# First block's gates and short convolution as pairs of seven half products, with x kept in memory meanwhile

## The chip, the cores and the metric

The program runs on one core of a Trainium2 chip. Its time is the device time of one execution in microseconds; of several executions the median is given. The engines are TensorE (PE: matmuls, with PEld for its weight loads), VectorE (DVE), ScalarE (ACT), GpSimd (POOL) and SyncE (SP), which here only issues transfers. Each engine runs its own instructions in order and waits for the others on semaphores.

## What is computed

Two transformer blocks of width 1024 over 1024 positions. The first block normalizes x, projects it (`w_in`) to the features of an RWKV-7 recurrence, of a short convolution and of two gates, and merges the two branches:

```python
out_a = rwkv7_branch(...)            # scan, then a group norm per head of 64, bonus, gate
u = cg * xc                          # short_conv_branch
out_b = bg * conv3(u, conv_w)        # causal, depthwise, width 3
merged = (sigmoid(ga + bg_a) * (out_a @ w_proj_a) + sigmoid(gb + bg_b) * (out_b @ w_proj_b))
x = x + merged @ w_out_mix
```

`ga` and `gb` have 1024 columns each, `bg`, `cg` and `xc` 512 each. Attention to a memory and an MLP follow, and then the second block.

## The kernel before

Activations lie transposed: a tile is 128 features by 1024 positions, in two halves of 512 (`HALF`). For precision every operand of a large product is split in two parts, `hi` (rounded) and `lo` (the remainder), and a product is three matmuls: hi by w_hi, lo by w_hi, hi by w_lo. A weight tile is 128 output columns by 1024 inputs (`KT` = 8 k-steps of 128), so a plain tile is 8 x 3 x 2 = 48 matmuls of 512 columns (`Weights.multiply`, line 280). GpSimd splits a weight tile (`split_tile`: `w_hi` at line 161, `w_lo` at line 164) after its transfer has landed and its slot is free.

In the first block the order is: features (`rwkv_features`, four turns of three tiles), the scan (`rwkv_scan`), and then the stage that changes. `gates` runs 16 plain tiles (for each of `ga` and `gb` eight) and applies the sigmoid out of PSUM (line 2744) to two buffers that are stored to memory. Its first tile is multiplied at the end of the scan's block (`multiply_early`). Beside it `RwkvOutput` finishes the scan's output in eight halves: TensorE sums over heads (lines 2412 and 2418, full precision), VectorE centres, takes a reciprocal (2445) and scales (2447 to 2455), ScalarE squares, takes the root (2430) and rounds. `ShortConv` follows in the same block: 12 plain tiles, in four turns of `cg`, `xc` and `bg`. Then `merge` multiplies both branches by their projections; its weights and the stored gates come in on the sync queue (`fetch`, `load_gates`, line 3277). `add_product` adds the last product to x, which stays in on-chip memory (`x_t`) all the time.

Other stages already use seven half products instead of eight for a pair of tiles (a Winograd form of Strassen's scheme): the MLP, and the second block's gates, `pair_gates`. There two tiles of 128 columns by 1024 inputs are a 2 x 2 block matrix with the halves of the inputs, as are the activations with the halves of the inputs and of the positions. Four sums of the activations' blocks are formed once (`HalfSums`: t1 on GpSimd, lines 2852 to 2860; t2, t3 and t4 on VectorE in PSUM, lines 2885 to 2895, rounded by ScalarE). Four sums of weight blocks per pair are formed by GpSimd (`sum_into`, line 823), every operand is rounded by ScalarE (`round`, line 807) and its remainder taken by GpSimd (`rest`, line 818) into a ring of five slots. A product is 4 k-steps x 3 = 12 matmuls (line 859), a pair 84. Between products ScalarE copies and VectorE adds partial results between PSUM banks (`seed_u`, `keep_fifth`, `seed_last`, `add_fifth`, `end_fifth`). `EarlyPart` multiplies just 2 of the 8 k-steps of the first tile before the block boundary.

Blocks (`nc.Block`) are separated by a barrier of all engines; semaphores can be cleared between them (`clear_and_free_semaphores`).

## Time and profile before

| what | us |
|---|---|
| median of 3 runs | 2989.02 (2986.13 to 2990.33) |
| profiled execution, its time | 2989.97 |
| its span, first to last instruction | 2988.2 |
| TensorE busy | 2863.9 |
| stage of gates and short convolution on TensorE | 499.83 to 819.94 |

The profile is of one execution. TensorE's mean granted clock in it is 0.989 of full speed. Times of rows are microseconds from the start of the span; a bracket gives the idle time before an instruction and who ended it.

### The profile page before, as it was taken

Reading aid. Unit: us, or ns where it says so; the run is one execution under the profiler, and the core shown is the slowest. Engines: PE = TensorE matmul, PEld = TensorE weight load, DVE = VectorE, ACT = ScalarE, POOL = GpSimd, SP = SyncE. Lnnn points to the kernel's source line nnn. Section 1 sums busy time; section 2 is a strip of 40 time slices with the busy share of each in tenths; the row PEclk is TensorE's granted clock in tenths of the full one; section 3 lists DMA queues with packets and bytes.
Section 4 is the critical chain, followed back from the end, with each engine's and each line's share of the span. In section 5 each row is a group of like instructions: output and inputs, shape, how many; then the busy total and the mean of one; then the engine's idle time right before and its main releaser. Section 6 shows DMA issues by size and latency. Waiting matters only on the chain. (4 is left out here: it accounts for less than half of the span.)

```text
span 2988.2 us, 48247 instructions
## 1 busy us (share of the span) xinstructions
PE 2863.9 (96%) x20146; PEld 2292.3 (77%) x20146; DVE 1476.3 (49%) x1739; ACT 950.9 (32%) x1455; POOL 1139.7 (38%) x807
## 2 busy tenths in 40 slices
PE   7999788999999999999999999999999799999999
PEld 6777677778878876788888888777877678866677
DVE  6454442423464434543333333777578436357661
ACT  5433232321011123422222222433233335567400
POOL 1331222444344430344444444211121457645552
PEclk9999999999999999999999999999999999999999
DMA  6232433442142111111111111122333534322143
GB/s 212 84 127 102 110 100 84 124 127 81 28 141 71 50 50 41 38 43 57 57 57 57 50 50 50 29 78 72 99 92 98 167 106 127 117 96 64 61 141 127
DMA packets 310864, 258.38 MB, mean 86 GB/s; under 512 B 47010, under 2 KB 269401, under 8 KB 310666
## 3 DMA queue, kind: packets, MB, share of 16 engines
q1 hardware_dynamic: 310410, 255.48, 28.3%
q8 instruction: 149, 2.44, 0.3%
q14 instruction: 49, 0.40, 0.0%
q10 hardware_dynamic: 256, 0.07, 0.0%
HBM read 191.79 MB, written 63.31 MB: 85 GB/s over the span
## 5 line engine op out<-in xcount | busy, mean ns | idle before, releaser
L280 PE MATMUL ps<-h_hi,w_hi 128*128 128x512 f32 x1376 | 444.2, 404 | 6.3 <-POOL w_lo L177 3.7
L280 PE MATMUL ps<-h_lo,w_hi 128*128 128x512 f32 x1376 | 426.4, 391 | 0.0
L280 PE MATMUL ps<-h_hi,w_lo 128*128 128x512 f32 x1376 | 425.1, 390 | 0.0
L161 POOL TENSOR_TENSOR w_hi<-w_raw,ones 128x1024 fp32r<-128x1024 f32 x78 | 189.3, 2427 | 475.8 <-PE ps L280 322.4
L818 POOL TENSOR_TENSOR op_lo<-w_raw,op_hi 128x512 fp32r<-128x512 f32 x160 | 205.8, 1291 | 371.8 <-ACT op_hi L807 371.2
L280 PEld LDWEIGHTS ps<-h_hi,w_hi 128*128 128x128 f32 x1376 | 256.7, 188 | 85.4 <-issue 31.0
L280 PEld LDWEIGHTS ps<-h_hi,w_lo 128*128 128x128 f32 x1376 | 259.4, 189 | 55.3
L280 PEld LDWEIGHTS ps<-h_lo,w_hi 128*128 128x128 f32 x1376 | 259.1, 188 | 55.3
L164 POOL TENSOR_TENSOR w_lo<-w_raw,w_hi 128x1024 fp32r<-128x1024 f32 x78 | 203.8, 2613 | 6.1
L1367 DVE TENSOR_TENSOR x_t<-x_t,ps 128x512 f32<-128x512 f32 x128 | 87.6, 687 | 223.2 <-PE ps L859 207.3
L177 POOL TENSOR_TENSOR w_lo<-w_raw,w_hi 128x1024 fp32r<-128x1024 f32 x30 | 73.1, 2438 | 303.6 <-ACT w_hi L172 303.6
L859 PE MATMUL ps<-hid_hi,op_hi 128*128 128x512 f32 x448 | 174.3, 389 | 0.0
L859 PE MATMUL ps<-hid_lo,op_hi 128*128 128x512 f32 x448 | 174.3, 389 | 0.0
L859 PE MATMUL ps<-hid_hi,op_lo 128*128 128x512 f32 x448 | 174.3, 389 | 0.0
L807 ACT CAST op_hi<-w_raw 128x512 fp32r<-128x512 f32 x155 | 95.6, 621 | 192.8 <-PE ps L859 158.2
L280 PE MATMUL ps<-branch_hi,w_hi 128*128 128x512 f32 x384 | 119.4, 392 | 5.8 <-POOL w_lo L164 2.1
L4561 DVE RECIPROCAL p_root<-p_root 128x1024 f32<-128x1024 f32 x16 | 104.8, 6547 | 36.3 <-ACT p_root L4415 36.1
L280 PE MATMUL ps<-branch_lo,w_hi 128*128 128x512 f32 x384 | 118.3, 389 | 0.0
L280 PE MATMUL ps<-branch_hi,w_lo 128*128 128x512 f32 x384 | 118.3, 389 | 0.0
L5389 POOL TENSOR_TENSOR sb_weight<-sb_weight,sb_left 128x512 f32<-128x512 f32 (+3 forms) x96 | 84.9, 896 | 71.2 <-DVE sb_left L5543 70.6
L5543 DVE TENSOR_TENSOR_SCAN sb_left<-ps,sb_left,ones 128x512 f32<-128x512 f32 (+3 forms) x96 | 92.4, 1004 | 34.2 <-ACT ps L5489 32.5
L859 PE MATMUL ps<-h_hi,op_hi 128*128 128x512 f32 x256 | 99.8, 390 | 0.0
(640 smaller groups left out, 5940.8 us busy)
## 6 DMA issues: line engine op xcount, KB each, us to landing
w_raw<-in_w_in_dram SPq DMA_DIRECT2D x91, 512.0 KB, 4.8
w_raw<-in_w_up_dram SPq DMA_DIRECT2D x32, 512.0 KB, 4.0
w_raw<-in_w_down_dram SPq DMA_DIRECT2D x32, 512.0 KB, 3.4
kv_raw<-in_w_kv_dram SPq DMA_DIRECT2D x16, 512.0 KB, 5.1
mix_gates<-mix_sig SPq DMA_DIRECT2D x16, 512.0 KB, 3.0
mix_gate_b<-mix_gates SPq DMA_DIRECT2D x32, 256.0 KB, 4.3
mix_gates<-mix_sig SPq DMA_DIRECT2D x32, 256.0 KB, 2.5
x_in<-in_x_dram SPq DMA_DIRECT2D x8, 512.0 KB, 8.9
```

The lines of the kernel that those rows point to most:

```text
L161: pool.tensor_tensor(c.w_hi[:, s], c.w_raw[:, s], c.ones[:].unsqueeze(1).broadcast_to([P, KT, P]), ALU.mult).then_inc(c.w_rounded, 1)
L164: pool.tensor_tensor(c.w_lo[:, s], c.w_raw[:, s], c.w_hi[:, s].bitcast(F32), ALU.subtract).then_inc(c.w_split, 1)
L177: eng.tensor_tensor(c.w_lo[:, s], c.w_raw[:, s], c.w_hi[:, s].bitcast(F32), ALU.subtract).then_inc(c.w_split, 1)
L280: last = pe.matmul(o, w[:, s, k], a[:, k - offset, (half + h) * width:(half + h + 1) * width], start=(k == kts[0] and w is c.w_hi and a is ...
L807: act.copy(self.hi(o)[:], src).then_inc(self.rounded, 1)
L818: pool.tensor_tensor(self.lo(o)[:], src, self.hi(o)[:].bitcast(F32), ALU.subtract).then_inc(self.pooled, 1)
L859: last = pe.matmul(out, w[:, k], a(k), start=start and k == 0 and w is w_hi and a is hi, stop=stop and k == HK - 1 and w is w_lo, skip_gro ...
L1367: dve.tensor_tensor(c.x[:, n, half[h]], c.x[:, n, half[h]], ps[:, bank_of(g, n, place)], ALU.add).then_inc(down_free, 1)
L4561: v.mark(dve.reciprocal(root[:], root[:]))
L5389: pool.tensor_tensor(weight[:, n % 4, hd, 0:width], weight[:, n % 4, hd, 0:width], left[:, n % 2, hd, 1:width + 1], ALU.mult).then_inc(wei ...
L5543: dve.tensor_tensor_scan(l[:, hd, 0:width][:, ::-1], ps[:, 2 * (n % 2) + hd, 0:width][:, ::-1], c.ones[:, 0:1].broadcast_to([P, width]), l ...
```

## The change

The 28 tiles of the stage become four plain gate tiles and 24 tiles in twelve pairs of seven half products, six pairs of gate tiles and six of convolution tiles (`cg` with `xc` twice, then two `bg` tiles, and all again). `first_gates` takes the place of `gates` and `ShortConv`. Its half sums t2 and t3 need the room of x, so x is stored to memory in the features stage (two tiles a turn, ahead of the turn's weight fetches) and loaded again during the merge's first turns; t1 is rounded in place of a quarter of the activations, once the last plain tile has read it (`h12_read`). The splits of t1 are issued within the first pair. The scan's output is finished beside the plain tiles (halves 0 and 1) and the six gate pairs (one half each). The taps' accumulator is in PSUM. The merge's block is preceded by a clearing of semaphores, and `add_product` waits for x tile by tile.

```diff
--- before.py
+++ after.py
...
                 weights.done(dve, k // 2, k % 2)
+                dve.wait_ge(c.x_back, 16 * (k + 1))
                 dve.tensor_tensor(c.x[:, k], c.x[:, k], c.ps[:, 2 * (k % 2):2 * (k % 2) + 2, :].rearrange("p b n -> p (b n)"),
                                   ALU.add).then_inc(free[k % 2], 1)
...
+                    for n in range(2 * i, 2 * i + 2):
+                        sp.dma_start(c.scratch["x_spill"][n], c.x[:, n]).then_inc(c.x_spilled, 16)
                     fetch(i, 0)
                     fetch(i, 1)
...
-class ShortConv:
...
-def gates(c, name, w_in, first_column, bias):
...
@@ -2816,7 +2601,10 @@
         self.rest(pool, o)
         self.sum_into(pool, s3, a21, a11, ALU.subtract, count + self.SUM1)
         self.sum_into(pool, s2, s3, a22, ALU.add, count + self.SUM4)
-        for m in (1, 2, 3, 4):
+        first_sums()
+        self.rest(pool, o + 1)
+        before_third()
+        for m in (2, 3, 4):
             self.rest(pool, o + m)
...
+            t[1] = [buf[:, 0:HK, HALF:SEQ] for buf in (c.h_hi, c.h_lo)]
+        self.raw = [c.nc.alloc_sbuf_tensor_at(f"{name}_t1raw{m}", [P, HALF], F32, offset=off) for m, off in enumerate(raw)]
...
+def first_gates(c, w_in, bias):
...
+    gate_tile_of, conv_tile_of = tile_of(w_in, RWKV_COLS + 3 * D_RWKV), tile_of(w_in, RWKV_COLS)
+    weights = EarlyPart(c, [lambda i, u=u: gate_tile_of(0, 1, u // 2 + (u % 2) * KT) for u in range(4)], 1)
...
+        x_base, tail_base = c.h_base - BRANCH, aux + 2 * BRANCH
+        gate_tiles = [gate_tile_of(0, 1, 2 * i + k + g * KT) for i in range(1, 4) for g in range(2) for k in range(2)]
+        conv_order = [(o, i) for two in range(2) for o, i in ((1, 2 * two), (2, 2 * two), (1, 2 * two + 1), (2, 2 * two + 1),
+                                                              (0, 2 * two), (0, 2 * two + 1))]
+        s = PairStream(c, "gate_op", gate_tiles + [conv_tile_of(0, 1, o * CT + i) for o, i in conv_order], ring=(0, 2, 1, 4, 3), shift=0)
+        n_gates, n_pairs = len(gate_tiles) // 2, s.pairs
+        t = HalfSums(c, name, {2: x_base, 3: x_base + 16384, 4: tail_base},
+                     [aux + 28672, aux + 30720, aux + BRANCH + 24576, aux + BRANCH + 26624], banks={3: 5, 2: 6, 4: 7}, inplace=True)
...
+        with nc.Block() as block:
...
+                s.fetch(sp, 2)
+                side.load(sp, 1)
+                store_tile(0)
+                sp.wait_ge(c.w_split, weights.t0 + 3)
+                s.fetch(sp, 0)
+                sp.wait_ge(c.w_split, weights.t0 + 4)
+                s.fetch(sp, 1)
+                store_tile(1)
...
+                for p in range(n_pairs):
+                    s.fetch(sp, 2 * p + 3)
+                    if p < n_gates:
+                        store_quarter(p, 0)
+                        side.load(sp, p + 3)
+                    s.fetch(sp, 2 * p + 4)
...
+            @block.gpsimd
+            def _(pool):
+                t.pool_form(pool, 0)
+                t.pool_form(pool, 1)
+                weights.split_tile(pool, 0, 2)
+                t.pool_form(pool, 2)
+                weights.split_tile(pool, 0, 3)
+                t.pool_form(pool, 3)
+                weights.done(pool, 0, 2)
+                def first_sums():
+                    for j in range(HK):
+                        t.pool_split(pool, j)
+                s.pool_products(pool, 0, first_sums, lambda: weights.done(pool, 0, 3))
+                for p in range(1, n_pairs):
+                    s.pool_products(pool, p)
...
+                for u in range(2):
+                    pool.wait_ge(s.used, s.total - 3 + 3 * u)
+                    following.split_tile(pool, 0, u)
+                following.ahead = 2
...
+                    out_banks = [ps[:, 2 * (u % 2)], ps[:, 2 * (u % 2) + 1]]
+                    weights.ready(pe, 0, u)
+                    wait(pe, gated, u - 1)
+                    if u == 0:
...
+                        weights.part(pe, out_banks, c.h_hi, c.h_lo, range(HK), u).then_inc(h12_read, 1)
+                        last = weights.part(pe, out_banks, c.h_hi, c.h_lo, range(HK, KT), u)
+                    else:
+                        last = weights.multiply(pe, u, out_banks, c.h_hi, c.h_lo, before=between(u))
+                    last.then_inc(c.tile_done, 1)
...
+                    if gates_now and p:
+                        side.pe_means(pe, n)
+                    if p == 0:
+                        pe.wait_ge(side.rooted, 2)
+                    elif p == n_gates:
+                        pe.wait_ge(side.rooted, 2 * CT)
+                    else:
+                        bank_free(0)
+                    s.product(pe, o, ps[:, A], *b11).then_inc(s.used, 1)
+                    if p:
+                        bank_free(1)
+                    else:
+                        pe.wait_ge(gated, 3)
+                    s.product(pe, o + 1, ps[:, E], *t.at(1), before=after_split(1)).then_inc(s.used, 1)
+                    if gates_now and p > 1:
+                        side.pe_spreads(pe, n)
+                    pe.wait_ge(xcopied, 3 * p + 1)
+                    s.product(pe, o + 2, ps[:, B], *t.at(2), start=False, before=after_split(2)).then_inc(s.used, 1)
...
+                        pe.wait_ge(t.split[3], HK)
+                        side.pe_means(pe, n)
+                    if p == 1:
+                        side.pe_spreads(pe, n)
+                    s.product(pe, o + 3, ps[:, A], *b21, start=False).then_inc(s.used, 1)
...
+                t.act_begin(act, 0)
+                t.act_round(act, 3, 0)
+                t.act_round(act, 2, 0)
+                t.act_round(act, 4, 0)
+                t.act_begin(act, 1)
+                gate_tile(0)
+                side.act_square(act, 0)
+                t.act_round(act, 3, 1)
+                t.act_round(act, 2, 1)
+                side.act_root(act, 0)
+                t.act_round(act, 4, 1)
+                t.act_begin(act, 2)
+                gate_tile(1)
+                side.act_late(act, 0)
+                side.act_square(act, 1)
+                t.act_round(act, 3, 2)
+                t.act_round(act, 2, 2)
+                t.act_round(act, 4, 2)
+                t.act_begin(act, 3)
+                side.act_root(act, 1)
+                gate_tile(2)
+                for m in (0, 1):
+                    s.round(act, m)
+                for j in range(HK):
+                    if j == 0:
+                        act.wait_ge(h12_read, 1)
+                    if j == HK - 1:
+                        t.act_round(act, 3, 3)
+                    act.wait_ge(t.formed[3], j + 1)
+                    t.act_round(act, 1, j)
+                t.act_round(act, 2, 3)
+                t.act_round(act, 4, 3)
+                weights.done(act, 0, 3)
+                s.round(act, 2)
+                gate_tile(3)
+                s.round(act, 3)
...
+                    o, n = s.PAIR_OPS * p, p + 2
+                    if p > 1:
+                        side.act_square(act, n)
+                    seed_u(p)
+                    s.round(act, o + 4)
+                    keep_fifth(p)
+                    if p == 1:
...
+                    s.round(act, o + 6)
+                    if p == 0:
+                        side.act_late(act, 1)
+                    gate_quarter(p, 0)
...
+                    if p:
+                        side.act_late(act, n)
+                    gate_quarter(p, 1)
+                    s.round(act, o + 9)
...
+                def add_fifth(p):
+                    A, E, B, C, DD = banks(p)
+                    dve.wait_ge(s.used, s.PAIR_OPS * p + 3)
+                    dve.wait_ge(xcopied, 3 * p + 2)
+                    if p <= n_gates:
+                        dve.wait_ge(gated, gates_until(p - 1, 2 if p else 3))
+                    else:
+                        dve.wait_ge(free[2], p - n_gates)
+                    dve.tensor_tensor(ps[:, C], ps[:, B], fifth[:], ALU.add).then_inc(xadded, 1)
...
+                        u, acc = u_in[h], ps[:, 6 + h]
+                        v.mark(dve.tensor_scalar(acc, u[:, 2:HALF + 2], vec(c, "conv_w", i + 2 * CT), None, ALU.mult))
+                        for tap in (1, 0):
+                            v.wait(dve)
+                            ins = dve.scalar_tensor_tensor(out=acc if tap else y[:, i, half[h]], in0=u[:, tap:HALF + tap],
+                                                           scalar=vec(c, "conv_w", i + tap * CT), in1=acc, op0=ALU.mult, op1=ALU.add)
+                            v.mark(ins)
+                    v.wait(dve)
+                    dve.sem_inc(ended, 1)
...
+                def gate_y(p, m):
+                    n, h, product = places[m]
+                    i = conv_at(p, n)[1]
+                    finished(p, m)
+                    dve.tensor_tensor(y[:, i, half[h]], y[:, i, half[h]], ps[:, bank(p, m)], ALU.mult).then_inc(made, 1)
+                    dve.wait_ge(made, 4 * ((p - n_gates) // 3) + m + 1)
+                    dve.sem_inc(free[m], 1)
...
+                dve.wait_ge(c.x_spilled, 16 * KT)
+                dve.memset(u_in[0][:, 0:2], 0.0).then_inc(padded, 1)
+                form(0, 3, 2, 4)
+                split_t(0, 3, 2, 4)
+                side.dve_centre(dve, 0)
+                form(1, 3, 2, 4)
+                split_t(1, 3, 2, 4)
+                side.dve_invert(dve, 0)
+                side.dve_apply(dve, 0)
+                side.dve_finish(dve, 0)
+                side.dve_centre(dve, 1)
+                form(2, 3, 2, 4)
+                split_t(2, 3, 2, 4)
+                form(3, 3, 2, 4)
+                split_t(3, 3, 2, 4)
+                side.dve_invert(dve, 1)
+                side.dve_apply(dve, 1)
+                for p in range(n_gates):
+                    n = p + 2
...
+                    if products_of(p):
+                        gate_y(p, 0)
+                        end_fifth(p)
+                        gate_y(p, 1)
+                        split_y(p, 0)
+                        gate_y(p, 2)
+                        split_y(p, 1)
+                        gate_y(p, 3)
+                        split_y(p, 2)
+                        split_y(p, 3)
+                    else:
+                        end_fifth(p)
+                        scale_u(p, 1)
+                        scale_u(p, 3)
+                        taps(p)
+    return weights, build
...
+            nc.clear_and_free_semaphores(c.done_with)
+            c.stage_sems = [s for s in c.stage_sems if s not in c.done_with]
         with nc.Block() as block:
...
                             fetch(i, u)
                         load_gates(i + 1, u)
+                        for k in range(4 * i + 2 * u, 4 * i + 2 * u + 2) if x_back and i < 2 else ():
+                            sp.dma_start(c.x[:, k], c.scratch["x_spill"][k]).then_inc(c.x_back, 16)
                 sp.wait_ge(c.w_split, weights.t0 + weights.total)
                 following.load_first(sp)
...
 def first_block(c):
     d = c.dram
+    scratch(c, "x_spill", [KT, P, SEQ])
     loras, lora_tail = start_to_loras(c)
+    c.x_spilled, c.x_back = c.sem("x_spilled"), c.sem("x_back")
     feature_weights, features = rwkv_features(c)
     loras(feature_weights)
     scan_in = ScanInputs(c)
     features(scan_in, lora_tail)
-    gate_weights, gate = gates(c, "mix", d["w_in"][0], RWKV_COLS + 3 * D_RWKV, "b_gate")
+    gate_weights, gate = first_gates(c, d["w_in"][0], "b_gate")
     rwkv_scan(c, gate_weights, scan_in)
     c.br_hi = at(c, 0, "branch_hi", [P, KT, SEQ], F32R)
     c.br_lo = at(c, BRANCH, "branch_lo", [P, KT, SEQ], F32R)
-    side = RwkvOutput(c)
     merge_weights, merge_1 = merge(c, "mix", d["w_proj_a"][0], d["w_proj_b"][0])
-    sig = [at(c, BRANCH + 4 * (CT + n) * SEQ, f"mix_sig{n}", [P, SEQ])[:] for n in range(2)]
-    gate(side, sig, after=ShortConv(c, side, merge_weights))
+    gate(merge_weights)
     out_weights = residual_weights(c, d["w_out_mix"][0])
-    merge_1(out_weights)
+    merge_1(out_weights, x_back=True)
     h, branches = (c.h_hi, c.h_lo), (c.br_hi, c.br_lo)
     query_weights, query = queries(c)
     late = LateNorm(c, "norm_xattn", query_weights, branches, "norm_xattn")
```

## Rows read from the trace of the kernel before

**Rows 1.** Page, busy us, share of the span, instructions.
```profile
PE 2863.9 (96%) x20146; PEld 2292.3 (77%) x20146; DVE 1476.3 (49%) x1739; ACT 950.9 (32%) x1455; POOL 1139.7 (38%) x807
```

**Rows 2.** Timeline of TensorE through the stage: start, us, engine, line, operation, count.
```profile
499.83 0.73 PE L280 MATMUL ps<-h_hi,w_hi 128*128 128x512 f32 x2
...
510.39 0.61 PE L280 MATMUL ps<-h_hi,w_lo 128*128 128x512 f32 x2
511.33 0.70 PE L280 MATMUL ps<-h_hi,w_hi 128*128 128x512 f32 x2 [0.32 <-PEq L1935]
...
642.69 1.04 PE L280 MATMUL ps<-h_hi,w_hi 128*128 128x512 f32 x2
643.56 0.62 PE L280 MATMUL ps<-h_lo,w_hi 128*128 128x512 f32 x2
...
718.85 0.62 PE L280 MATMUL ps<-h_hi,w_lo 128*128 128x512 f32 x2
...
730.18 0.62 PE L280 MATMUL ps<-h_hi,w_hi 128*128 128x512 f32 x2
...
819.94 0.62 PE L280 MATMUL ps<-branch_hi,w_hi 128*128 128x512 f32 x2
```

**Rows 3.** Busy time by stretch (columns in the first line), one pair, second gates.
```profile
core 0: us, PE busy (x) PEld busy (x) DVE busy (x) ACT busy (x) POOL busy (x), PEclk, DMA share, GB/s
2560.20:2581.10 20.90, 20.90 (x101) 17.54 (x100) 7.45 (x10) 12.34 (x19) 14.37 (x11) 1.00 0.43 127
```

**Rows 4.** Timeline of TensorE, boundary before the second block's gates.
```profile
2469.83 0.70 PE L2909 MATMUL ps<-h_hi,w_hi 128*128 128x512 f32 x2 [1.00 <-PEq L4750]
```

**Rows 5.** Timeline of VectorE and GpSimd, half sums of the second gates.
```profile
2470.43 0.70 DVE L2887 TENSOR_TENSOR ps<-ps,h_lo 128x512 f32<-128x512 f32 x1 [3.80 <-ACT ps L2865]
...
2476.78 0.68 DVE L2895 TENSOR_TENSOR mix_t4lo<-ps,mix_t4hi 128x512 fp32r<-128x512 f32 x1
...
2483.26 2.54 POOL L2860 TENSOR_TENSOR mix_t1lo<-mix_t1raw,mix_t1hi 128x512 fp32r<-128x512 f32 x2
```

**Rows 6.** Timeline of ScalarE and VectorE, first half of the scan's output.
```profile
519.26 1.28 ACT L2430 ACT_TABLE_LOAD   x1
...
522.52 3.35 DVE L2445 RECIPROCAL ro_root<-ro_root 128x512 f32<-128x512 f32 x1 [6.37 <-ACT ro_root L2430]
525.91 1.71 DVE L2447 TENSOR_TENSOR ro_dev<-ro_dev,ro_root 128x512 f32<-128x512 f32 x1
527.66 2.50 DVE L2449 TENSOR_SCALAR ro_dev<-ro_dev,vec 128x512 f32<-128x512 f32 x1
```

**Rows 7.** Timeline of TensorE behind a wait in the memory keys.
```profile
72.45 0.73 PE L3599 MATMUL ps<-kv_hi,mem_hi 128*128 128x512 f32 x2 [2.43 <-DVE kv_lo L3589]
...
77.36 0.61 PE L3599 MATMUL ps<-kv_hi,mem_lo 128*128 128x512 f32 x2
```

**Rows 8.** Busy time by stretch, the same place.
```profile
74.00:76.00 2.00, 2.00 (x6) 1.52 (x6) 2.00 (x3) 0.71 (x2) 0.00 (x0) 0.50 1.19 297
```

**Rows 9.** Timeline of SyncE, GpSimd and TensorE, the merge's fifth tile.
```profile
855.26 0.38 SPq L124 DMA_DIRECT2D w_raw<-in_w_proj_a_dram  x1
...
861.02 2.39 POOL L161 TENSOR_TENSOR w_hi<-w_raw,ones 128x1024 fp32r<-128x1024 f32 x1 [13.31 <-DMA w_raw<-in_w_proj_b_dram]
863.49 2.39 POOL L164 TENSOR_TENSOR w_lo<-w_raw,w_hi 128x1024 fp32r<-128x1024 f32 x1
...
866.13 0.70 PE L280 MATMUL ps<-branch_hi,w_hi 128*128 128x512 f32 x2 [0.77 <-DVE mix_gate_a L3351]
```

**Rows 10.** DMA view of 848 to 866 us, in 40 slices.
```profile
GB/s 0 0 27 123 314 269 173 341 373 378 300 32 0 0 214 355 305 305 296 337 328 249 307 340 325 133 22 93 264 223 109 178 173 319 287 264 273 296 346 344
DMA packets 3522, 4.06 MB, mean 225 GB/s; under 512 B 239, under 2 KB 1985, under 8 KB 3521
```

**Rows 11.** Waits of TensorE, whole span: us in total, times, longest.
```profile
PE ps L4305 <- PEq L5558: 1.6, 1, 1.6
```

**Rows 12.** Waits of TensorE, 2500 to 2642 us.
```profile
PE ps L2498 <- ACT do_sq L2490: 0.8, 1, 0.8
```

**Rows 13.** Groups by shape, 497 to 865 us: busy us, mean ns; idle before.
```profile
L2634 DVE TENSOR_TENSOR branch_lo<-conv_y,branch_hi 128x512 f32 x6 | 12.4, 2105 | 1.2 <-ACT branch_hi L2600 1.2
```

554 lines of the change are left out of this document (323 added, 231 removed).

## Prediction

> **What bounds the kernel now.** I read the engine shares first: TensorE is busy for 96% of the span, so time is won by giving it less work and lost wherever it is made to wait [rows 1]. Then I read its timeline through the stage that changes. The stage starts at 499.83 us, when the first gate tile is multiplied behind the scan, and ends at 819.94 us, when the merge's first product starts: 320.1 us [rows 2]. Between 718.85 and 730.18 us there are 50 matmuls of 512 columns, so one costs 0.2266 us. The stage has 28 tiles (16 gate, 12 convolution) of 8 k-steps, 3 products and 2 halves: 1344 matmuls, 304.6 us. The 16 full-precision sums of the scan's output cost more: the pair that holds one takes 0.87 us instead of 0.45, and the sum itself 0.45, so 0.87 each, 13.9 us. One block boundary adds 0.49 us (510.39 + 0.45 to 511.33). Together 319.0 of 320.1 us: TensorE never waits here for another engine. Third, the second block's gates: they already run as plain tiles and then six pairs of seven half products, which makes them the measured model of the new stage.
>
> **What the change removes.** Four plain tiles are 192 matmuls; 24 tiles in 12 pairs are 12 x 7 products x 4 k-steps x 3 = 1008. That is 1200 in place of 1344: 144 fewer at 0.2266 = **-32.6 us**. The 16 sums stay.
>
> **Whether the pairs keep pace.** A pair of the other gate stage takes 20.90 us with TensorE busy throughout, 84 x 0.2266 = 19.0 plus its side work; GpSimd is busy for 14.4 us of it, ScalarE 12.3, VectorE 7.5 [rows 3]. The new gate pairs last 19.0 + 2 x 0.87 = 20.8, the convolution pairs 19.0. GpSimd's eleven operations (7 remainders, 4 sums; 14.37 / 11 = 1.3 us each) fit either. In a gate pair VectorE gets a 3.35 us reciprocal and about 3 to 6 us of scaling where the model had 0.2 us; that is about 12 of 20.8 us, and the bank it releases last (the fifth quarter) is wanted only three products (8.2 us) later. A convolution pair gives VectorE six tap operations; their accumulator lies in PSUM, where operations took 0.70 us beside GpSimd [rows 5], so about 5 us, over before the next pair's addition is due at 8.2 us. I cost the 12 pairs at no stall; if the cover were gone, each microsecond per pair would be 12 us.
>
> **The start of the stage.** Until now a whole tile (10.9 us) was multiplied before the block boundary and covered it. Now only 2 of 8 k-steps are (12 matmuls, 2.7 us), as in the other stage, where TensorE waited 1.00 us at the boundary [rows 4] against 0.32 here; the last store of the scan must land as well, so I take **+1.0** rather than 0.7 (bounds 0.6 to 2).
> After it (call this T) TensorE has 36 + 144 matmuls and four sums, so pair 0 could begin at T+44.3. VectorE has to form and split the half sums in that time. In the model one of four rounds took 7.05 us (2470.43 to 2477.46) [rows 5], so 28 us. But it also has two halves of the scan's output to finish: a reciprocal of 3.35 us and four scalings, of which the first two took 1.71 and 2.50 us while GpSimd worked [rows 6]. I walk the written order with these durations: sums 0 until T+8; centring 0 at 9.3, behind TensorE's sum; sums 1 until 19.0, because ScalarE's root with its 1.28 us table load stands between its roundings; reciprocal until 22.4; scaling beside GpSimd until 29.5; finishing and centring 1 until 32.2; sums 2 until 39.4; sums 3 until 44.5. ScalarE waits for these: its last `act_begin` ends at 39.1, root 1 at 41.1, the gate of tile 2 with another table load at 43.5, the rounding of weight 0 at 44.1. Only then can GpSimd go on: remainder 0 (45.4), two sums (48.0), **four splits of the first half sum, now inside the first pair** (two took 2.54 us in the model [rows 5], so 5.1; 53.0), remainder 1 (54.3). TensorE begins product 0 at 45.4, is done at 48.1 and waits for remainder 1 until 54.3. Against a start at T+44.3 and product 1 at 47.0 this is 7.3 us, of which about 0.6 is the second spread sum waiting for ScalarE's square. The walk takes the slowed scalings at their slowest, so I take **+6.5** (bounds: 1, if VectorE's scalings are not slowed and ScalarE gains what it loses to table loads; 12).
> A wait of that kind has an after-effect in this trace: behind a 2.43 us wait the granted clock went from full to 0.50 (1.2 GHz), and 14 matmuls took 4.91 us instead of 3.17 [rows 7, 8]. **+1.7** (0 to 3).
> What else is queued there: product 2 needs the second half sum (split by 47) and its seed copy (51), so nothing is late next; the first pair's addition meets a VectorE that is still scaling until about 58, when product 2 ends at 60.
>
> **The copies of x.** Eight stores of 512 KB in the features stage go on the sync queue ahead of weight fetches whose tile is due a whole turn (three tiles) later: 0. Reading back is another matter. The sync queue issues two loads of 512 KB (x0, x1) after the gate loads of tile 2 of the merge and two more (x2, x3) just ahead of the weights of tile 4, which before were issued at 855.26, landed at 861.0, were split by 865.88, and TensorE started on them at 866.13: it was already waiting for exactly this chain [rows 9]. In that stretch the DMA engines moved 4.06 MB in 18 us with few free slots, 300 to 340 GB/s when backed up [rows 10]. Another 2 MB is 6.5 us of transfer, less some 1.7 us of free slots: **+4.8 us** on tile 4; tile 6 meets x6 and x7 in the same way, about +0.2 after that. I take **+5.0** (0 to 8). This wait could cool the clock as well; I put this in the range.
> The Trainium skill, "DMA: Bandwidth & Descriptors", section "Queues, rings and completion order", says that each DMA engine takes the descriptors of one queue in ring order. By it what was issued first is paid for in full before the weights land, which gives +4.8; did the engines share, it would be nearer 2.4. No row of before has an x load in front of a weight, so neither is shown.
> The addition of x later waits for loads issued 30 us earlier: 0.
>
> **The merge's boundary.** The first merge tile still covers the barrier (its wait there before was as short as the one at 511.33), but its semaphores are now cleared between the blocks. Where that happens alone TensorE waited 1.6 us [rows 11]: **+1.3** (0 to 2).
>
> **Sum.** -32.6 + 1.0 + 6.5 + 1.7 + 5.0 + 1.3 = -17.1. The profiled execution took 2989.97 us (span 2988.2 and 1.8 around it), 0.95 above the median of the runs, 2989.0. So 2972.9 beside the profiled one, **2972 us** as a median.
>
> **Rivals.**
> 1. *The start fits.* If ScalarE and VectorE run as smoothly as in the model, where TensorE waited just 0.8 us up to the end of the pairs [rows 12], GpSimd reaches remainder 1 about when it is wanted. For: VectorE's forming operations read PSUM and kept 0.70 us beside GpSimd. Against: the model split its first half sum before the pairs. -32.6 + 1.0 + 1 + 5.0 + 1.3 = -24.3: 2964.7; with the x loads hidden as well 2959.7.
> 2. *The x loads are hidden*, as the weights find a free slot or the merge lags anyway: -17.1 - 5.0 = -22.1, 2966.9.
> 3. *The pairs don't keep pace; slower.* In a gate pair ScalarE stands in order behind VectorE's scaling (`act_late`), and every later rounding of weights behind it. If the slowed scalings (1.71 and 2.50 us) pushed `act_late` past the next pair's start, each gate pair would lengthen. Against: the chain ends about T'+21.5 and the bank is wanted at 24.4, 2.9 us spare. It decides from 2.9 us per gate pair (17.1 / 6), and tells as slower above 3.9 us: at 5 us, 30 - 17.1 = +12.9, 3001.9.
> 4. *The convolution pairs stall on VectorE's split of y*, which took 2.1 us each beside GpSimd before [rows 13]: there are two pairs with four such splits, and at 4 us a pair it is +8: 2980.
>
> **How the numbers follow.** 0.2% is 6 us, about what a measurement of this kernel can tell from no change. Forecast (both waits there) 0.50; rival 1 0.18; rival 2 0.17; rival 4 0.07; rival 3 0.08, half of it mild. Forecast's own range: 2966 to 2981. Taking in rivals 1 and 2 and the upper bounds (12 instead of 6.5 at the start, 8 instead of 5 in the merge, a cold clock there too): 2960 to 2984. Faster by over 0.2% (below 2983): all but the upper end and rival 3, 0.91; within 0.2%: 0.05; slower: 0.04.
>
> **What would show it.** In the profile after: 1200 matmuls in the stage; pairs 1 to 11 at 20.8 (gates) and 19.0 us (convolution) with TensorE waiting for nothing; one wait of 5 to 7 us ahead of the second product of pair 0, released by GpSimd's remainder (line of `rest`), a granted clock of 0.5 just behind it; a wait of 4 to 6 us at the merge's fifth tile, released by GpSimd's `w_lo` behind a DMA; 1.5 to 2 us at the merge's boundary. I would be wrong if the pairs show repeated waits, or if the waits at the start and in the merge are missing or twice as long.

## Result, and the profile after

| | us |
|---|---|
| before, median of 5 runs | 2989.02 (2982.85 to 2990.33) |
| after, median of 5 runs | 2970.28 (2964.78 to 2975.13) |
| ratio | 0.9941, 95% interval 0.9924 to 0.9958 |
| profiled execution after, its time | 2970.81 |
| its span | 2969.1 |

The change makes the kernel faster by 18.7 us, 0.6%. The prediction gave 2972 us.

I read the profile after in the order of the prediction. First the engine shares: TensorE has 28.8 us less to do than in [rows 1], VectorE 44 us more and GpSimd 86 us more.

```profile
PE 2835.1 (95%) x20002; PEld 2268.7 (76%) x20002; DVE 1520.3 (51%) x1800; ACT 1029.1 (35%) x1607; POOL 1225.6 (41%) x907
```

Then TensorE's timeline through the stage and the merge, to be held against [rows 2, 9] (start, length, engine, line, operation, count; in brackets the idle time before it and who ended it):

```profile
503.03 0.73 PE L2699 MATMUL ps<-h_hi,w_hi 128*128 128x512 f32 x2
...
506.68 0.70 PE L2699 MATMUL ps<-h_hi,w_hi 128*128 128x512 f32 x2 [0.64 <-PEq L1938]
...
540.25 1.10 PE L2436 MATMUL ps<-ro_sq,ones 128*128 128x512 f32 x2 [0.66 <-ACT ro_sq L2431]
...
552.45 0.47 PE L860 MATMUL ps<-h_hi,gate_op_hi 128*128 128x512 f32 x1 [0.21 <-POOL gate_op_lo L819]
...
561.60 0.77 PE L860 MATMUL ps<-h_hi,gate_op_hi 128*128 128x512 f32 x1 [6.17 <-POOL gate_op_lo L819]
562.16 0.63 PE L860 MATMUL ps<-h_lo,gate_op_hi 128*128 128x512 f32 x1
...
799.86 0.62 PE L280 MATMUL ps<-branch_hi,w_hi 128*128 128x512 f32 x2
...
811.22 0.71 PE L280 MATMUL ps<-branch_hi,w_hi 128*128 128x512 f32 x2 [0.32 <-PEq L2778]
...
850.00 1.20 PE L280 MATMUL ps<-branch_hi,w_hi 128*128 128x512 f32 x2 [5.66 <-POOL w_lo L164]
850.99 1.06 PE L280 MATMUL ps<-branch_lo,w_hi 128*128 128x512 f32 x2
```

The stage lasts from 503.03 to 799.86 us, 296.8 us instead of 320.1. It has one long wait, 6.17 us ahead of product 1 of pair 0 (pairs, products, remainders and tiles are counted from 0). The merge has another, 5.66 us at its fifth tile, tile 4; it lasts 96.9 us where it took 90.7. At the merge's boundary the wait is 0.32 us, what a boundary cost before.

The busy times by stretch show what lies behind and between (in order: the stretch, its length, busy time and instructions of PE, PEld, DVE, ACT and POOL, TensorE's granted clock, DMA share, GB/s). The first and last stretch follow the two waits; between them one gate pair and one convolution pair:

```profile
561.50:565.00 3.50, 3.40 (x8) 2.75 (x9) 3.43 (x3) 0.00 (x0) 3.50 (x3) 0.52 0.00 0
585.00:605.90 20.90, 20.90 (x90) 16.57 (x89) 14.31 (x12) 12.92 (x21) 13.96 (x11) 1.00 0.40 118
...
700.00:719.00 19.00, 19.00 (x86) 15.73 (x85) 7.37 (x11) 6.63 (x13) 12.99 (x11) 1.00 0.23 57
...
850.00:855.00 5.00, 5.00 (x12) 3.98 (x13) 1.60 (x3) 0.63 (x1) 3.53 (x2) 0.50 0.65 195
```

The pairs last what was predicted, TensorE busy throughout. Behind both waits the granted clock is at its lower level, 1.2 GHz.

Who ended the first wait: GpSimd's timeline. It idles 10.07 us until ScalarE rounds the first weight, and then does remainder 0, two weight sums, four splits of t1 and remainder 1 in one go, up to 561.49:

```profile
551.00 1.29 POOL L819 TENSOR_TENSOR gate_op_lo<-w_raw,gate_op_hi 128x512 fp32r<-128x512 f32 x1 [10.07 <-ACT gate_op_hi L808]
552.26 2.66 POOL L824 TENSOR_TENSOR w_raw<-w_raw 128x512 f32<-128x512 f32 x2
554.88 4.95 POOL L2650 TENSOR_TENSOR h_lo<-mix_t1raw,h_hi 128x512 fp32r<-128x512 f32 x4
559.77 1.72 POOL L819 TENSOR_TENSOR gate_op_lo<-gate_op_sum,gate_op_hi 128x512 fp32r<-128x512 f32 x1
```

And the second: SyncE issues two loads of x at 829.44 and two at 834.84, and then the weights of tile 4. GpSimd begins to split them 8.2 us after their second part was issued. In the kernel before that took 5.3 us (861.02 in [rows 9], issued at 855.69, the first line here, which is of the kernel before):

```profile
855.69 0.51 SPq L124 DMA_DIRECT2D w_raw<-in_w_proj_b_dram  x1
```
```profile
829.44 0.91 SPq L3599 DMA_DIRECT2D x_t<-x_spill  x2
...
834.84 0.91 SPq L3599 DMA_DIRECT2D x_t<-x_spill  x2
...
836.47 0.81 SPq L124 DMA_DIRECT2D w_raw<-in_w_proj_b_dram  x1
...
844.66 2.35 POOL L161 TENSOR_TENSOR w_hi<-w_raw,ones 128x1024 fp32r<-128x1024 f32 x1 [16.70 <-DMA w_raw<-in_w_proj_b_dram]
847.08 2.67 POOL L164 TENSOR_TENSOR w_lo<-w_raw,w_hi 128x1024 fp32r<-128x1024 f32 x1
```

Outside the change two differences stay. The stage begins 3.2 us later, and from the attention's first product to the end the profile is 5.2 us shorter (1892.8 against 1898.0 us). Together: +3.2 - 23.3 + 6.2 - 5.2 = -19.1, the difference of the spans. Neither is the change's as far as the runs show: over the twelve profiles of this document that last length lies between 1889.2 and 1898.0 us, and the start of the stage varies in the same way (see below).

### The profile page after: what moved, and what is told of

Same layout as the page of the kernel before. It is cut to its first block and busy times, and to the rows that moved or that the text cites. A ratio compares the mean times of both kernels' runs of the same rounds, so it can differ in the third digit from the quotient of the medians.

```text
span 2969.1 us, 48063 instructions
## 1 busy us (share of the span) xinstructions
PE 2835.1 (95%) x20002; PEld 2268.7 (76%) x20002; DVE 1520.3 (51%) x1800; ACT 1029.1 (35%) x1607; POOL 1225.6 (41%) x907
## 5 line engine op out<-in xcount | busy, mean ns | idle before, releaser
L280 PE MATMUL ps<-h_hi,w_hi 128*128 128x512 f32 x960 | 310.8, 405 | 6.4 <-POOL w_lo L177 3.7
L280 PE MATMUL ps<-h_lo,w_hi 128*128 128x512 f32 x960 | 297.5, 391 | 0.0
L280 PE MATMUL ps<-h_hi,w_lo 128*128 128x512 f32 x960 | 296.5, 390 | 0.0
L161 POOL TENSOR_TENSOR w_hi<-w_raw,ones 128x1024 fp32r<-128x1024 f32 x54 | 132.5, 2454 | 297.8 <-PE ps L280 178.1
L280 PEld LDWEIGHTS ps<-h_hi,w_hi 128*128 128x128 f32 x960 | 178.9, 189 | 63.8 <-issue 24.8
L280 PEld LDWEIGHTS ps<-h_lo,w_hi 128*128 128x128 f32 x960 | 181.0, 189 | 38.8
L280 PEld LDWEIGHTS ps<-h_hi,w_lo 128*128 128x128 f32 x960 | 180.8, 188 | 38.8
L177 POOL TENSOR_TENSOR w_lo<-w_raw,w_hi 128x1024 fp32r<-128x1024 f32 x30 | 75.1, 2502 | 302.4 <-ACT w_hi L172 302.4
L164 POOL TENSOR_TENSOR w_lo<-w_raw,w_hi 128x1024 fp32r<-128x1024 f32 x54 | 145.5, 2694 | 4.2
L4868 DVE RECIPROCAL p_root<-p_root 128x1024 f32<-128x1024 f32 x16 | 104.7, 6546 | 36.9 <-ACT p_root L4722 36.7
```

The source lines that it names most:

```text
L161: pool.tensor_tensor(c.w_hi[:, s], c.w_raw[:, s], c.ones[:].unsqueeze(1).broadcast_to([P, KT, P]), ALU.mult).then_inc(c.w_rounded, 1)
L164: pool.tensor_tensor(c.w_lo[:, s], c.w_raw[:, s], c.w_hi[:, s].bitcast(F32), ALU.subtract).then_inc(c.w_split, 1)
L177: eng.tensor_tensor(c.w_lo[:, s], c.w_raw[:, s], c.w_hi[:, s].bitcast(F32), ALU.subtract).then_inc(c.w_split, 1)
L280: last = pe.matmul(o, w[:, s, k], a[:, k - offset, (half + h) * width:(half + h + 1) * width], start=(k == kts[0] and w is c.w_hi and a is ...
L4868: v.mark(dve.reciprocal(root[:], root[:]))
```

## The experiments

Most comparisons below are of three lengths in the profile, since a median of five runs moves by 2 or 3 us: the stage (its first product to the merge's), the merge (to the next product's first matmul), and the time of the stage's start. The product and the query that follow took 179.5 to 179.6 us in all twelve profiles. Each length is read from one profile. How far they can be trusted shows where the code is the same: the stage took 296.8, 297.4, 296.5 and 296.6 us in the four kernels that leave it as in the changed one, the merge 96.9, 96.4 and 96.7 us in three.

| kernel | median us | ratio to before, 95% | stage starts | stage | merge |
|---|---|---|---|---|---|
| before | 2989.0 | | 499.8 | 320.1 | 90.7 |
| after | 2970.3 | 0.9941 (0.9924 to 0.9958) | 503.0 | 296.8 | 96.9 |
| before_with_x_stores | 2986.0 | 0.9999 (0.999 to 1.0008) | 499.8 | 320.0 | 90.1 |
| before_with_x_copies | 2996.9 | 1.0026 (1.0015 to 1.0037) | 503.3 | 320.0 | 96.4 |
| round_first | 2965.3 | 0.9913 (0.99 to 0.9927) | 505.8 | 291.9 | 96.4 |
| early_rounds | 2962.6 | 0.9914 (0.9899 to 0.9929) | 501.8 | 290.1 | 96.7 |
| fill_waits | 2964.3 | 0.9922 (0.9909 to 0.9935) | 498.9 | 295.1 | 92.9 |
| x_one_slot_later | 2967.5 | 0.9931 (0.9916 to 0.9945) | 503.2 | 297.4 | 95.2 |
| x_behind_weights | 2965.4 | 0.9913 (0.99 to 0.9927) | 505.4 | 296.5 | 90.1 |
| x_in_the_gap | 2961.7 | 0.9921 (0.9907 to 0.9934) | 501.4 | 296.6 | 90.8 |
| early_rounds_x_in_the_gap | 2959.9 | 0.9911 (0.9896 to 0.9926) | 501.7 | 290.8 | 92.0 |
| early_rounds_x_in_two_gaps | 2964.6 | 0.9912 (0.9896 to 0.9929) | 506.2 | 290.1 | 91.2 |

The kernel before ran beside each group: 2989.25, 2987.4 (before_with_x_stores, early_rounds, x_in_the_gap and the two together) and 2991.2 us (the last two tried); so ratios compare better than medians.

### round_first: ScalarE's order at the start

```diff
                 t.act_begin(act, 3)
-                side.act_root(act, 1)
-                gate_tile(2)
+                weights.done(act, 0, 2)
                 for m in (0, 1):
                     s.round(act, m)
-                for j in range(HK):
-                    if j == 0:
-                        act.wait_ge(h12_read, 1)
-                    if j == HK - 1:
-                        t.act_round(act, 3, 3)
+                act.wait_ge(h12_read, 1)
+                for j in range(HK - 1):
                     act.wait_ge(t.formed[3], j + 1)
                     t.act_round(act, 1, j)
+                side.act_root(act, 1)
+                gate_tile(2)
+                t.act_round(act, 3, 3)
+                act.wait_ge(t.formed[3], HK)
+                t.act_round(act, 1, HK - 1)
```

> Only ScalarE's order at the start changes: the roundings of the first two weight operands and of the first three quarters of t1 come ahead of the second root and the third gate tile (both with a table load of 1.28 us). Theory 1 (the 6.2 us wait ahead of product 1 of pair 0 is GpSimd's chain of remainder, two sums, four splits and remainder, which begins late because ScalarE rounds late): GpSimd's first remainder starts at about 546.6 instead of 551.0, its second ends at about 555.5 to 556, so TensorE waits 0 to 1 us instead of 6.2 and its clock stays full: 6 to 7.5 us less in the stage, total about 2963.5. Rival (the wait is set by GpSimd and VectorE slowing each other, or by the half sums formed late, so the chain only stretches): the wait stays above 4 us and the total changes by under 2 us.

The wait ahead of product 1 fell from 6.17 to 1.92 us and the stage by 5.0 us. Expected were a wait of 0 to 1 us and a gain of 6 to 7.5. Counted from the stage's start, remainder 0 begins 43.3 us in (expected 43.6, after 48.0), and remainder 1 ends 53.4 us in (52.5 to 53 expected, 58.5 after). TensorE and GpSimd in this kernel:

```profile
559.33 0.47 PE L860 MATMUL ps<-h_hi,gate_op_hi 128*128 128x512 f32 x1 [1.92 <-ACT mix_sig L2943]
```
```profile
549.06 1.30 POOL L819 TENSOR_TENSOR gate_op_lo<-w_raw,gate_op_hi 128x512 fp32r<-128x512 f32 x1 [5.68 <-ACT gate_op_hi L808]
...
557.95 1.28 POOL L819 TENSOR_TENSOR gate_op_lo<-gate_op_sum,gate_op_hi 128x512 fp32r<-128x512 f32 x1
```

The bracket names ScalarE's sigmoid, but that ended at 555.4. What ends at 559.23, 0.1 us ahead of the matmul, is GpSimd's remainder. So the chain on GpSimd set the wait, and what it starts earlier (4.7 us) the stage gains (5.0). The chain still ended 1.9 us too late, and slow matmuls stood behind even this short wait (granted clock 0.57 from 559.4 to 563 us).

### early_rounds: the same, further

```diff
                 side.act_square(act, 1)
+                weights.done(act, 0, 2)
+                for m in (0, 1):
+                    s.round(act, m)
                 t.act_round(act, 3, 2)
...
                 t.act_begin(act, 3)
-                side.act_root(act, 1)
-                gate_tile(2)
-                for m in (0, 1):
-                    s.round(act, m)
+                act.wait_ge(h12_read, 1)
                 for j in range(HK):
-                    if j == 0:
-                        act.wait_ge(h12_read, 1)
-                    if j == HK - 1:
-                        t.act_round(act, 3, 3)
                     act.wait_ge(t.formed[3], j + 1)
                     t.act_round(act, 1, j)
+                side.act_root(act, 1)
+                gate_tile(2)
+                t.act_round(act, 3, 3)
```

> Only ScalarE's order at the start changes, further than before: the two weight roundings go into its idle time ahead of the third round of half sums, and all four roundings of t1 ahead of the second root and the third gate tile. Theory 1 (GpSimd's chain, ended by the remainder that product 1 wants, sets the wait): its first remainder and two sums fall into GpSimd's idle time, the four splits start about 46 us after the stage's start and the second remainder ends at about 53, when product 0 still runs: no wait over 0.5 us, no low clock, the stage 288.5 to 289.5 us instead of 296.8, total about 2962. Rival (VectorE's and GpSimd's shared pace or the late root gives a wait of the same size elsewhere in pair 0): the stage stays above 292 us.

The wait is gone, and with it the low clock (1.00 from 550 to 560 us). GpSimd does remainder 0 and the two sums in what was idle time; the splits begin 44.2 us into the stage and remainder 1 ends 50.5 us in, while TensorE multiplies product 0:

```profile
539.33 1.30 POOL L819 TENSOR_TENSOR gate_op_lo<-w_raw,gate_op_hi 128x512 fp32r<-128x512 f32 x1
...
546.01 5.04 POOL L2650 TENSOR_TENSOR h_lo<-mix_t1raw,h_hi 128x512 fp32r<-128x512 f32 x4 [2.76 <-ACT h_hi L2659]
551.00 1.31 POOL L819 TENSOR_TENSOR gate_op_lo<-gate_op_sum,gate_op_hi 128x512 fp32r<-128x512 f32 x1
```

The stage takes 290.1 us, 6.7 less than in the changed kernel. Expected were 288.5 to 289.5; one microsecond came back as three short waits in pairs 0 and 1 (0.48, 0.24 and 0.29 us), of which this is the largest (VectorE scales the scan's output ahead of the pair's addition):

```profile
563.08 0.50 PE L860 MATMUL ps<-mix_t3hi,gate_op_hi 128*128 128x512 f32 x1 [0.48 <-DVE ps L3111]
```

### fill_waits: is the low clock the price of standing idle?

```diff
+                        for _ in range(FILL_START):
+                            pe.matmul(ps[:, E], c.h_hi[:, 0, 0:P], c.h_hi[:, 0, half[0]], start=True, stop=True)
                     s.product(pe, o + 1, ps[:, E], *t.at(1), before=after_split(1)).then_inc(s.used, 1)
...
+                        if isinstance(i, int) and i == 2 and u == 0:
+                            for _ in range(FILL_MERGE):
+                                pe.matmul(c.ps[:, b], c.br_hi[:, 0, 0:P], c.br_hi[:, 0, 0:HALF], start=True, stop=True)
+                            weights.ready(pe, i, u)
```

(Both constants are 22. The second part stands in place of the wait for these weights further up; TensorE's turns of the merge, a loop otherwise, are written out.)

> The changed kernel with 22 more matmuls of 512 columns (5.0 us at full clock) in each of the two long waits, into the bank that the next product starts anew: they use only what is there already, so they end before the wait would. Theory 1 (the low clock behind the waits comes from TensorE standing idle): the granted clock stays at full behind both, and the stage and the merge are each 1.5 to 2 us shorter than in the changed kernel; total about 2966.5 to 2967.5. Rival (the clock falls for another reason, or the cost behind the waits is operands that come late): the matmuls behind the waits stay slow, no gain, or up to 1 us of loss where the filling outlasts the wait.

TensorE in this kernel, at the start of the pairs and at the merge's fifth tile:

```profile
550.87 5.15 PE L2907 MATMUL ps<-h_hi 128*128 128x512 f32 x22
557.27 0.50 PE L861 MATMUL ps<-h_hi,gate_op_hi 128*128 128x512 f32 x1 [1.25 <-POOL gate_op_lo L820]
557.60 0.39 PE L861 MATMUL ps<-h_lo,gate_op_hi 128*128 128x512 f32 x1
...
838.34 5.15 PE L3625 MATMUL ps<-branch_hi 128*128 128x512 f32 x22
843.33 0.73 PE L280 MATMUL ps<-branch_hi,w_hi 128*128 128x512 f32 x2
843.90 0.62 PE L280 MATMUL ps<-branch_lo,w_hi 128*128 128x512 f32 x2
```

At the first place the real products start nearly where they did (58.3 us into the stage against 58.6; the wait at the block boundary was 0.30 us in this profile, 0.64 in the other), but run at 0.23 us each instead of 0.43. From product 1's start to product 2's it is 2.85 us instead of 4.34. So of the 1.7 us that the stage is shorter 1.5 are the low clock. In the merge 4.0 us went. The first 46 matmuls of tile 4 took 2.3 us less, which is the clock; 0.9 is that the tile begins earlier (49.3 us into the merge against 50.1), which may be the turns written out and was not tried by itself; 0.6 is a wait at the merge's end that is gone. At these two places an idle TensorE was dearer than the wait that is read in the bracket.

### before_with_x_stores and before_with_x_copies: one part of the change alone

The second is the kernel before with the stores, the loads and the wait of `add_product` (the lines that the change adds for them). The first has only the eight stores and, in the merge, SyncE's wait for them.

> The kernel before with one part of the change alone: x is stored in the features stage and loaded in the merge at the changed kernel's places, and the last product waits for it; nothing else is changed. Theory 1 (the copies cost nothing where they are stored, and about 5 to 7 us in the merge with the cold clock, whatever stands ahead of it): 2994 to 2996, with a wait of 5 to 6 us at the merge's fifth tile. Rival A (the merge's wait comes from the pairs, which leave the first gate loads or weights late): at most 2 us more than before, about 2990. Rival B (the stores disturb the features or the scan too, where the changed kernel's stage begins 3.2 us later than before): the stage of gates also begins about 3 us later, 2997 to 3000.

> The kernel before with the eight stores of x alone; nothing is loaded back and nothing waits for it. Open is why the changed kernel's stage began 3.2 us later. Theory 1 (it is the length of the low clock at the start of the scan, which varies from run to run: with the same stores one run began its stage at 498.9 us and four at 503 to 506): the median is within 1.5 us of before, about 2989.5. Rival (the stores ahead of the weights delay something in the features or the scan): 2992 to 2993.

With the loads the merge takes 96.4 us, 5.7 more than before and as much as in the changed kernel, with the same wait at its fifth tile:

```profile
873.94 1.19 PE L280 MATMUL ps<-branch_hi,w_hi 128*128 128x512 f32 x2 [5.43 <-POOL w_lo L164]
```

So the merge's loss is the loads', and the pairs have no part in it (rival A falls). This profile's stage too began 3.5 us late, which spoke for rival B. The stores alone settled it: ratio 0.9999 (0.999 to 1.0008), stage starting at 499.8. A cost of 3.2 us would be a ratio of 1.0011. The stage starts of the twelve profiles lie between 498.9 and 506.2 us, and kernels with the same stores are found at 498.9, 499.8 and 506.2. So it varies from one execution to the next. It does so within the scan: the scan's first matmul comes at 300.3 to 302.2 us in all twelve, behind the stage with the stores, and from there to the gates it is 198.5 to 205.5 us. My explanation by the length of the low clock at the scan's start does not hold: the kernel with the stores alone had the clock at 0.77 from 320 to 330 us, lower than the changed kernel (0.87), and was early (the first line is the stores' kernel, the second the changed one). What varies there stays open.

```profile
320.00:330.00 10.00, 7.94 (x187) 7.08 (x184) 5.58 (x12) 2.44 (x5) 0.00 (x0) 0.77 0.22 50
```
```profile
320.00:330.00 10.00, 7.80 (x209) 6.72 (x208) 5.63 (x12) 3.00 (x6) 0.00 (x0) 0.87 0.27 60
```

### x_one_slot_later, x_behind_weights, x_in_the_gap: what the loads cost where

```diff
 x_one_slot_later
-                        for k in range(4 * i + 2 * u, 4 * i + 2 * u + 2) if x_back and i < 2 else ():
+                        for k in range(4 * i + 2 * u - 2, 4 * i + 2 * u) if x_back and 0 < 2 * i + u < 5 else ():
                             sp.dma_start(c.x[:, k], c.scratch["x_spill"][k]).then_inc(c.x_back, 16)
 x_behind_weights
                             fetch(i, u)
+                        for k in range(4 * i + 2 * u - 2, 4 * i + 2 * u) if x_back and 1 < 2 * i + u < 5 else ():
+                            sp.dma_start(c.x[:, k], c.scratch["x_spill"][k]).then_inc(c.x_back, 16)
                         load_gates(i + 1, u)
-                        for k in range(4 * i + 2 * u, 4 * i + 2 * u + 2) if x_back and i < 2 else ():
+                        for k in range(2) if x_back and i == 0 and u == 0 else ():
 x_in_the_gap
                             fetch(i, u)
+                        for k in range(KT) if x_back and i == 2 and u == 0 else ():
+                            sp.dma_start(c.x[:, k], c.scratch["x_spill"][k]).then_inc(c.x_back, 16)
                         load_gates(i + 1, u)
-                        for k in range(4 * i + 2 * u, 4 * i + 2 * u + 2) if x_back and i < 2 else ():
-                            sp.dma_start(c.x[:, k], c.scratch["x_spill"][k]).then_inc(c.x_back, 16)
```

> Only the places of x's eight loads in the merge change: each pair of loads is issued one tile later, so that two (x0, x1) and not four stand ahead of the weights of tile 4, and x6, x7 come behind those of tile 5. Theory 1 (the weights of tile 4 wait for all that was issued ahead of them on the same queue): 1 MB less ahead of them, the wait of 5.8 us falls by 2.5 to 3.3 us and the cold clock behind it shrinks with it; the loads then stand ahead of the weights of tile 5, which may wait 0 to 2 us; total 2 to 4 us less, about 2967. Rival (the engines share their transfers among what is open, or tile 4 is late for another reason): the wait stays within 1 us of 5.8.

> Only the order within each turn of the merge's transfers changes against the changed kernel: x0 and x1 stay, the other three pairs of loads are issued right behind the weights of tiles 4, 5 and 6 instead of right ahead of them. The open question is whether transfers of one queue are served in the order of issue. Theory 1 (in order): the weights of tile 4 land as in the kernel before and the wait of 5.8 us falls to under 1.5 us, the merge to 90 to 92 us, total about 2965. Rival (what is open at once is served together, so the place within 1 us of issue does not matter): the wait stays at 4 to 6 us, the merge at 95 to 97 us.

> Only the places of x's loads in the merge change: all eight are issued behind the weights of tile 6, where the transfers stood still for some 12 us (about 60 to 72 us after the merge's start). Theory 1 (what costs is what is issued in the few microseconds ahead of a weight; there x comes behind the weights and ahead of gates that are wanted 10 us later): the merge takes 90 to 91.5 us instead of 96.9, total about 2964.5. Rival (4 MB more in the merge cost their 6 us wherever they stand): a wait of 3 to 6 us moves to tile 6 or 7, and the merge stays at 94 to 97 us.

The number to compare is when GpSimd can begin to split tile 4. It and the issue of the weights' second part are counted from the merge's start:

| kernel | loads of x ahead of the weights | weights issued | split of tile 4 begins | wait at tile 4 |
|---|---|---|---|---|
| before | none | 35.8 | 41.1 | 0.77 |
| after | two 6.4 us ahead, two just ahead | 36.6 | 44.8 | 5.66 |
| x_one_slot_later | two just ahead | 36.7 | 44.1 | 4.67 |
| x_behind_weights | two 5.5 us ahead, two just behind | 35.2 | 41.4 | 2.16 |
| x_in_the_gap | none | 33.7 | 39.2 | none over 0.3 |

Moving x0 and x1 out of the way gave 0.7 us, not the 2.5 to 3.3 that I expected of "1 MB less ahead": issued at 829.44 us, they landed at 834.8 and 836.5, when the weights had just been issued. Moving x2 and x3 from just ahead of the weights to just behind them, by 0.8 us of issue time, gave 3.4 us. In x_behind_weights SyncE, GpSimd and TensorE show:

```profile
837.15 0.51 SPq L124 DMA_DIRECT2D w_raw<-in_w_proj_b_dram  x1
837.70 0.98 SPq L3598 DMA_DIRECT2D x_t<-x_spill  x2
```
```profile
843.34 2.39 POOL L161 TENSOR_TENSOR w_hi<-w_raw,ones 128x1024 fp32r<-128x1024 f32 x1 [13.58 <-DMA w_raw<-in_w_proj_b_dram]
```
```profile
848.41 0.70 PE L280 MATMUL ps<-branch_hi,w_hi 128*128 128x512 f32 x2 [2.16 <-POOL w_lo L164]
```

The transfers land in the order of issue. In the changed kernel x2 and x3 land at 841.2 and 842.8 us and the weights' second part at 844.5; in x_behind_weights the weights land at 843.2 and x2 and x3, issued 0.5 us behind them, at 844.5 and 845.8. The times from issue to landing, of x2 and the weights in the changed kernel, and of the weights and x2 in this one:

```profile
x_t<-x_spill SPq DMA_DIRECT2D x1, 512.0 KB, 6.4
w_raw<-in_w_proj_b_dram SPq DMA_DIRECT2D x1, 256.0 KB, 8.0
```
```profile
w_raw<-in_w_proj_b_dram SPq DMA_DIRECT2D x1, 256.0 KB, 6.0
x_t<-x_spill SPq DMA_DIRECT2D x1, 512.0 KB, 6.8
```

Not all of the 3.4 us is transfer time, though. The last gate load ahead of the weights landed 40.2 us into the merge in the changed kernel and 39.5 in this one, which is 0.7 us. From there to the weights it was 4.4 us with x2 and x3 between and 1.7 us without (1.5 in the kernel before, where nothing was issued for 3.6 us behind them). So the 1 MB itself took 2.7 us, about 380 GB/s. The remaining wait of 2.16 us is hardly a loss against before: TensorE reaches this tile 1.1 us earlier than it did (44.3 against 45.4 us into the merge), as a wait of 0.88 us at the third tile is gone. The merge takes 90.1 us, expected 90 to 92.

x_in_the_gap uses the same order at the other end. The eight loads stand behind the weights of tile 6, where almost nothing was transferred (DMA shares of 0.10, 0.00 and 0.17 in the three stretches of 4 us from 860 to 872 us of the profile after). Tile 4 no longer waits; its split begins 1.9 us earlier than before, as its weights were issued 2.1 us earlier. But tile 7 waits, whose weights now have 4 MB ahead of them: the eight loads landed one after the other, 1.3 us apart, the last at 868.2 us, and the weights at 872.7. The merge takes 90.8 us, expected 90 to 91.5:

```profile
877.69 0.73 PE L280 MATMUL ps<-branch_hi,w_hi 128*128 128x512 f32 x2 [2.55 <-POOL w_lo L164]
```

### The version with both

> Both of the last two edits. Theory 1 (the two waits are independent): both gains add, about -14 us against the changed kernel, 2956 to 2957.5. Rival (an earlier start only moves the merge into a busier moment of the transfers, or a part of either gain was the run's own variation): less than 11 us of gain, above 2959.

> Both edits, with x's eight loads parted: four behind the weights of tile 6 and four behind the gates of tile 7, so that 2 MB less stand ahead of the weights of tile 7, which came late with eight. Theory (the waits of 2.3 to 2.7 us at tile 7 were those 2 MB too many): no wait over 1 us in the merge, which takes 88 to 90 us; the stage 290 to 291 us as with the early rounds; total 2956 to 2958. Rival (the last four loads now delay the weights of the product that follows, or its last tiles wait for x): a new wait of 2 us or more behind the merge, no gain against 2959.9.

From the stage's start to the attention's first product these take 562.3 and 560.9 us, the changed kernel 573.3 and the kernel before 590.4. So the two edits come to 11.0 and 12.4 us; expected were 14 for the first, and under 11 us, or a median above 2959, by its rival. Measured were 11.0 and 2959.9, so the gains did not add in full (alone, over the same stretch, they are 6.8 and 6.5 us). The first one's stage is 0.7 us longer than that of early_rounds, and behind its wait of 2.33 us at tile 7 the clock fell to 0.57, where x_in_the_gap kept it full behind 2.55 us, and the merge took 1.2 us more (first line x_in_the_gap, second this one):

```profile
877.70:882.00 4.30, 4.30 (x19) 3.57 (x20) 3.67 (x6) 1.24 (x2) 0.27 (x1) 1.00 0.76 213
```
```profile
872.00:876.00 4.00, 4.00 (x11) 3.13 (x12) 3.54 (x6) 1.24 (x2) 0.27 (x1) 0.57 0.81 223
```

Parting the loads removed tile 7's wait, but waits for gates came in its place, 1.42 us at tile 4 and this one at the merge's end:

```profile
887.55 0.70 PE L280 MATMUL ps<-h_hi,w_hi 128*128 128x512 f32 x2 [1.80 <-DVE mix_gate_b L3659]
```

The merge took 91.2 us, expected 88 to 90, and the median was 2964.6, expected 2956 to 2958. By their ratios (0.9911 and 0.9912, with intervals of about 0.003) the two can't be told apart, nor surely from early_rounds or x_in_the_gap alone. They are 26 to 27 us faster than the kernel before; against the changed kernel the difference of the ratios gives 9 us, with intervals that just overlap, and the profiled lengths 11 to 12.

## Why the prediction was right

**The products.** -32.6 us: confirmed. The trace after has 192 matmuls in plain tiles and 1008 in pairs between 503 and 800 us, and gate pairs of 20.9 and convolution pairs of 19.0 us without a wait. Rivals 3 and 4 fall: VectorE is busy for 14.3 of 20.9 us in a gate pair, more than the 12 that I had reckoned, and still not late; the splits of y between 740 and 800 us took 0.89 us on the mean, not the 2.1 of [rows 13].

**The boundary ahead of the pairs.** +1.0 was too much: 0.3 in this profile, and 0 to 0.3 in the others. The model's 1.00 [rows 4] was not the right row; 2.7 us of products cover the boundary nearly as well as a whole tile.

**The start.** The walk through the written order gave 7.3 us against the schedule without waits and the sum took +6.5. The three waits of the trace are 6.17 + 0.66 + 0.21 = 7.0. Place, releaser and chain are as walked, and round_first and early_rounds show that the chain on GpSimd, held back by ScalarE's order, is the cause. Rival 1 (the start fits) falls. The walk itself was better than the value that I took from it; my doubt about the slowed scalings concerned VectorE, which did not end the wait.

**The low clock behind it.** +1.7 predicted, 1.5 measured by filling the wait.

**The loads of x.** That the chain behind the weights sets this tile's start was read rightly: the bracket in [rows 9] names VectorE, but the product begins 0.25 us after `w_lo` ends, there as in the kernels with longer waits. +5.0: the wait grew by 4.9 us, and before_with_x_copies shows that the loads alone do it; rival 2 falls. The size came out partly by luck. I charged all four loads (2 MB, less free slots). In fact the split began 3.7 us later, and most of that is the two loads just ahead of the weights: moving them alone gave 3.4 us, moving the others alone 0.7. The rest of the 4.9 is a slower split (0.2) and TensorE reaching the tile 0.9 us earlier. The Trainium skill, "DMA: Bandwidth & Descriptors", section "Queues, rings and completion order", has each DMA engine take the descriptors of one queue in ring order. x_behind_weights agrees (41.4 against 44.8 us, and the landings above), and an equal sharing does not fit.

**The merge's other terms.** Semaphore clearing: +1.3 predicted, 0.0 measured (0.32 us of wait, as before): cleared between blocks they cost nothing here, where a tile of products covers the boundary. Left out of the sum was a low clock behind this wait too, 2.3 us, though I had taken it at the start from [rows 7, 8] and the same rows held here. And I did not see that the wait at the third tile would go, -0.9. The three errors are +1.3, -2.3 and +0.9 (predicted less measured): they cancel by luck, so that +6.3 met +6.2.

**The sum.** -17.1 predicted from the stage's start to the attention, -17.1 in the profiles. The agreement to a tenth is better than the method: four terms were off by 0.7 to 2.3 us. The medians differ by 18.7; the 1.6 us more lie outside the two stages, where profiles of like code differ by more than that.

## What to carry to other kernels

Where a long wait is expected, add what TensorE's clock loses behind it (1.5 us on 6.2 and 2.3 on 5.7 here), in each place. On the queue that was backed up here 1 MB took 2.7 us from the weights issued right behind it and next to nothing from those issued right ahead, so bulk loads with a late deadline belong behind the weights, and into stretches where the transfers stand still. When one engine's late start sets a wait, look for what stands ahead of its releaser in the written order that nobody needs yet: here a root and a sigmoid with their table loads, 4.3 us, ahead of two roundings.

## What the runs showed of the hardware

- The length of a wait alone doesn't tell whether the clock falls. It fell (0.50 to 0.57) behind waits of 6.17, 5.66, 4.67, 2.33 and 1.92 us, and stayed full behind 2.55, 2.16, 1.80 and 1.42 us. In the other profiles too it fell behind every wait over 4 us. What tells them apart stays open. Busy with products of no use, TensorE kept its full clock across the two long ones.
- One queue's transfers landed in the order of issue: 1 MB of loads landed ahead of the weights when issued 1 us ahead of them (842.8 and 844.5 us) and behind them when issued 0.5 us behind (845.8 and 843.2 us). Eight loads of 512 KB in a row landed 1.3 us apart.
- The start of the stage behind the scan varied by 7 us (498.9 to 506.2) between profiles of kernels that differ little up to there but for the eight stores, more than most of the edits are worth. Lengths from one landmark to the next told 1 us; whole medians did not tell 3.
